# Hybrid decoder step on one core: gate tanh staged in three buffers, and the next weight block's low half made behind the first gate piece

## The reference, cut to what matters

```python
h = rmsnorm(x, norm_pre)
p = h @ w_in                               # 1088 tokens (1024 prompt, 64 sample), 3624 columns
y_conv = conv3(p.conv_c * p.conv_h)        # causal, depthwise, width 3, 256 channels
o_conv = p.conv_b * y_conv * silu(p.conv_z)
out = concat[nsa(p) * silu(z_nsa), gla(p) * silu(z_gla), o_conv] @ w_out
x = x + rmsnorm(out, norm_post)
```

## Time and profile before

| what | value |
|---|---|
| median of 3 runs | 958.06 us |
| lowest and highest | 951.75 and 960.32 us |
| span of the profiled execution, first to last instruction | 956.0 us |
| PE busy | 906.1 us (95% of the span) |
| DVE, ACT, POOL busy | 588.0, 421.0, 191.8 us |
| projection stage within the span | 0 to about 285 us |

### The profile page before, as it was taken

One profiled execution on the slowest core, in us unless ns is written; L12 is line 12 of the kernel. 1 busy time (PEld: TensorE's weight loads), 2 busy tenths in 40 slices (PEclk: granted clock), 3 DMA queues, 4 the chain that ended last, 5 costly groups with the idle time before them and its releaser, 6 DMA issues. The chain is left out here.

```text
span 956.0 us, 16677 instructions
## 1 busy us (share of the span) xinstructions
PE 906.1 (95%) x5935; PEld 796.0 (83%) x5935; DVE 588.0 (62%) x1396; ACT 421.0 (44%) x932; POOL 191.8 (20%) x179
## 2 busy tenths in 40 slices
PE   5999999997999999999999999997789999999997
PEld 4999999997989999988999998886355667777765
DVE  6432010058345567898866668897487788788663
ACT  6432221111113556777645657774373344434322
POOL 0029499999701000000000033000000000000000
PEclk9999999998998999999999999999698999999999
DMA  7227534543305211000011010431435365551411
GB/s 251 73 89 212 232 110 135 164 133 122 94 25 162 71 46 47 9 1 1 1 40 53 21 49 16 121 99 57 173 108 140 107 191 163 148 167 56 148 52 34
DMA packets 106820, 93.73 MB, mean 98 GB/s; under 512 B 21245, under 2 KB 99954, under 8 KB 104626
## 3 DMA queue, kind: packets, MB, share of 16 engines
q1 hardware_dynamic: 84946, 58.65, 20.5%
q10 hardware_dynamic: 19488, 17.25, 5.9%
q0 software_dynamic: 2304, 16.78, 5.1%
HBM read 78.16 MB, written 18.61 MB: 101 GB/s over the span
## 5 line engine op out<-in xcount | busy, mean ns | idle before, releaser
L660 PE MATMUL ps<-w_hi,h_hi 128*128 128x264 f32 (+5 forms) x432 | 124.1, 287 | 0.2 <-DVE h_lo L532 0.2
L660 PE MATMUL ps<-w_lo,h_hi 128*128 128x264 f32 (+5 forms) x432 | 123.1, 285 | 0.0
L660 PE MATMUL ps<-w_hi,h_lo 128*128 128x264 f32 (+5 forms) x432 | 123.0, 285 | 0.0
L540 DVE TENSOR_TENSOR w_lo<-w_raw,w_hi 128x1024 fp32r<-128x1024 f32 (+3 forms) x13 | 34.4, 2648 | 127.6 <-ACT w_hi L434 127.6
L1469 DVE TENSOR_REDUCE least<-ps 128x1 f32<-128x640 f32 (+7 forms) x128 | 89.8, 703 | 24.9 <-PE ps L1297 23.7
L1473 DVE TENSOR_TENSOR pt_lo<-ps,pt_hi 128x512 fp32r<-128x512 f32 x132 | 89.9, 686 | 17.2 <-ACT pt_hi L1405 15.6
L1405 ACT ACTIVATE pt_hi<-ps 128x512 fp32r<-128x512 f32 x132 | 78.2, 596 | 44.9 <-PE ps L1310 39.7
L381 POOL TENSOR_TENSOR chunk<-chunk 128x1024 f32<-128x1024 f32 (+2 forms) x46 | 82.4, 1792 | 3.6
L660 PEld LDWEIGHTS ps<-w_hi,h_hi 128*128 128x128 f32 (+1 forms) x432 | 79.7, 185 | 0.6 <-issue 0.4
L660 PEld LDWEIGHTS ps<-w_lo,h_hi 128*128 128x128 f32 (+1 forms) x432 | 79.8, 185 | 0.0
L660 PEld LDWEIGHTS ps<-w_hi,h_lo 128*128 128x128 f32 (+1 forms) x432 | 79.5, 184 | 0.0
(11 more groups left out here) (378 smaller groups left out, 2219.5 us busy)
## 6 DMA issues: line engine op xcount, KB each, us to landing
kv_pages<-in_cache_slc_kv SPq DMA_DIRECT2D x256, 64.0 KB, 1.9
shared<-in_x_prompt SPq DMA_DIRECT2D x8, 512.0 KB, 3.5
w_raw<-in_w_in SPq DMA_DIRECT2D x8, 512.0 KB, 3.9
wr_raw<-in_w_in SPq DMA_DIRECT2D x8, 512.0 KB, 4.3
kv_window<-in_cache_win_kv SPq DMA_DIRECT2D x4, 1024.0 KB, 5.8
wo_raw<-in_w_out SPq DMA_DIRECT2D x8, 512.0 KB, 8.4
out<-in_cache_win_kv SPq DMA_DIRECT2D x1, 4032.0 KB
x_row<-in_x_prompt ACTq DMA_DIRECT2D x7, 512.0 KB, 4.6
```

Of the source, the lines that this page charges most:

```text
L540: nc.vector.tensor_tensor(half(w_lo, b), raw(b), half(w_hi, b).bitcast(F32), ALU.subtract).then_inc(s_wlo, 1)
L660: mm = nc.tensor.matmul(out, lhs, rhs, start=(k == 0 and i == 0), stop=(k == KD - 1 and i == 2))
```

## The change

Three edits:

1. The tile `tanh` with its two buffers is gone. ACT writes tanh(z/2) into the three buffers of `stage`, by n % 3 of the gate piece n (0 to 5), and DVE works on it there.
2. ACT's wait: gate pieces 3 to 5 wait for the piece three before. Pieces 0 to 2 wait for all nine stores of block 5 out of that buffer (three each).
3. DVE's order in a block: for a z block only the first piece stands ahead of `split(b + 2)`, and the other two behind it. For h and b blocks the order stays. There are two z blocks, 8 and 12; a block 14 does not exist, so only block 8 has such a split, that of block 10.

```diff
--- before.py
+++ after.py
@@ -233,7 +233,6 @@
         w_lo = sb("w_lo", [P, 2, KD * WMAX], F32R)
         chunk = sb("chunk", [P, 2, CHT * 2 * ROW])
         stage = sb("stage", [P, 3, 364])
-        tanh = sb("tanh", [P, 2, 364])
         shared = sb("shared", [P, 3 * D])
         g_col = sb("g_col", [P, KD])
         stat = sb("stat", [P, 4])
@@ -458,9 +457,11 @@
                     elif what == "z":
                         t0, tn = CH3[t]
                         n = gate_no[x]
-                        if n >= 2:
-                            wait_taken(act, gates[n - 2])
-                        nc.scalar.activation(tanh[:, n % 2, 0:tn], ps[:, bank(x), 0:tn], ACT.Tanh, scale=0.5
+                        if n >= 3:
+                            wait_taken(act, gates[n - 3])
+                        else:
+                            act.wait_ge(s_st[n], 16 * ((len(staged) - n + 2) // 3))
+                        nc.scalar.activation(stage[:, n % 3, 0:tn], ps[:, bank(x), 0:tn], ACT.Tanh, scale=0.5
                                              ).then_inc(s_tanh, 1)
 
                 nc.scalar.preload_act_table_set("sqrt_and_others")
@@ -567,10 +568,10 @@
                     else:
                         n = gate_no[x]
                         dve.wait_ge(s_tanh, n + 1)
-                        did(nc.vector.scalar_tensor_tensor(tanh[:, n % 2, 0:tn], tanh[:, n % 2, 0:tn], 1.0, src,
+                        did(nc.vector.scalar_tensor_tensor(stage[:, n % 3, 0:tn], stage[:, n % 3, 0:tn], 1.0, src,
                                                            ALU.add, ALU.mult))
                         nc.vector.scalar_tensor_tensor(y_t[:, t0:t0 + tn], y_t[:, t0:t0 + tn], 0.5,
-                                                       tanh[:, n % 2, 0:tn], ALU.mult, ALU.mult
+                                                       stage[:, n % 3, 0:tn], ALU.mult, ALU.mult
                                                        ).then_inc(s_td, 1)
 
                 def conv(h):
@@ -617,12 +618,14 @@
                     if b == NB - 1:
                         dve.wait_ge(s_ct, 3)
                         nc.vector.tensor_copy(pq[HD:P, NT, 0:P], ps[HD:P, 7, 0:P]).then_inc(s_cn, 1)
-                    if b >= NTB:
-                        for x in prods:
-                            if x[0] == b and taken[x][0] == "dve":
-                                take(x)
+                    mine = [x for x in prods if x[0] == b and taken[x][0] == "dve"]
+                    first = 1 if kind(b) == "z" else len(mine)
+                    for x in mine[:first]:
+                        take(x)
                     if b + 2 < NB:
                         split(b + 2)
+                    for x in mine[first:]:
+                        take(x)
                     if kind(b) == "h":
                         conv(CHAN[b - NTB][1])
                     elif kind(b) == "b":
```

## The result

The changed kernel takes 948.67 us in the median of 9 runs (945.20 to 953.43), the kernel before 955.70 in 9 (951.21 to 960.32). The forecast's time was 950.2 us. The profiled execution has a span of 948.1 us, the number the sum gave, and a time of 949.82 us; so what lies around the span is 1.7 us.

The account below looks back on a forecast made before the run. TensorE, busy 95% of the span, was taken as the bound, so gains lay in its standstill and slow clock at block 10: −5.2 − 2.7 = −7.9 us, from 958.06 to 950.2 us; range 945.0 to 957.5.

Parts of the forecast that it names:

- the sum: Whole launch: span 956.0 − 7.9 = 948.1 us; from the median, 958.06 − 7.9 = 950.2 us, or −0.8%.
- The place and the size of the loss: TensorE at block 10, late in the projection: 5.2 us standstill plus 2.7 us slow clock, together 7.9 us, would go.
- the slow stretch: Behind the standstill, 232.6 to 238.8 us, TensorE's granted clock is 0.50, costing 2.7 us.
- Both parts are needed: Three tanh buffers ready block 10's high half by 217.3 us; the new order puts its split behind the first gate piece.
- The new wait for the stores of block 5: On ACT, the first gate pieces' tanh waits for stores issued before blocks 6 and 7; taken as 0 us.
- The split's end: VectorE's low half of block 10 ends at 225.2 us, at latest 226.8, ahead of TensorE's need at 227.5.
- What is late next: Block 11's split ends at 237.8 us, 1.7 to spare; the second convolution ends at 262 to 263.5, needed at 263.8.
- The wait that shrinks but stays: Rival, chance 0.14: block 10's split falls behind POOL's multiply, ends 1.8 us too late; 952.0 us, or 954.7 with slow clock.
- No loss in most launches: Rival, chance 0.15: engine order varies by launch, some have no gap at block 10; median 957 to 959 us.
- The convolution as the bound: Rival, chance 0.07: second convolution beside POOL takes 13.8 us, TensorE waits 6.4 before block 13, loses 2.7 to clock; 959.3 us.

Follow-up runs that it names:

- one copy more: Changed kernel with one PSUM copy of 364 elements between the first gate piece and block 10's split; no TensorE wait, stage ends at 277.29 us.
- the runs with a delayed split: Changed kernel with three or seven PSUM copies of 364 elements between the first gate piece and block 10's split; ratios to before 0.9939 and 0.9968.
- GpSimd late: Changed kernel with 13 memsets of 1024 elements on GpSimd ahead of its step 13; ratio to before 1.0055, stage ends at 286.54 us.

## Why the prediction was right

*The place and the size of the loss.* Right. 5.2 us of standstill and 2.7 of slow clock were foretold to go; the stage ended 8.2 us earlier. Of that, 0.15 us is a last block a little shorter (its last piece is taken 3.85 us behind the one before instead of 4.00); against the second profile of the kernel before it was 7.4 us, so how much of the slow stretch falls on matmuls is a thing of the single launch.

*Both parts are needed.* The text gave each its reason, and the two runs with one half each bore it out: a wait of 4.9 us with the buffers alone, 2.2 with the order alone, none with both. The new wait for the stores of block 5, taken at 0, cost nothing: the first tanh starts at 207.81, before at 207.80.

*The split's end.* Right by 0.3 us: 224.93 against 225.2. The reading behind it, that POOL's small add holds it and the gather issue then waits, is what the rows show (1.67 us for the issue). A smaller reading was wrong: the issue of 1.96 us at 211.81 was put down to the long convolution step, but that step starts at 213.15; the one beside it was the step before, from 211.63 to 212.91.

*What is late next.* I had 1.7 us to spare at block 11. There were 4.5: its split ended at 234.98, wanted at 239.5, since it came between two of POOL's adds and took 1.21 us, where I had taken 3.37. This time POOL was the one to wait: its three adds took 6.04 us there, 5.55 before. The second convolution ended at 261.4, where I had 262 to 263.5.

*The wait that shrinks but stays.* It did not happen in the two profiles of the changed kernel nor with one copy more. Its price was about right in the launch and a little low in its wait: the runs with a delayed split gave 2.2 and 2.4 us where I had 1.8, and ratios of 0.994 and 0.997, 952 to 955 us on the forecast's scale. The 1.8 came of counting the gather issue and the multiply from 223.4; by the earlier trace rows the multiply ends at 228.95, and a split behind it at 230.2, 2.7 us too late. The slow stretch, when it came, cost 1.7 us and not 2.7.

*No loss in most launches.* This rival falls. PE's wait was there in both profiles of the kernel before and in the buffers alone, at the same place and length. The spread of one kernel's times comes from elsewhere: the later stages took 670.9 and 666.5 us in two profiles of the changed kernel, with all of the projection alike.

*The convolution as the bound.* It was right that this decides the sign: with GpSimd late the launch took 1.0055 of the time before. The price I put on it was too low: 15.8 us of convolution where I had 13.8, and 7.4 us of wait where I had 6.4.

*The measured gain* of 7.0 us between medians is a little under the 7.9 of the profiles. The median of the kernel before fell from 958.06 in the 3 runs shown to 955.70 in 9 (954.57 and 954.80 in the 31 and 19 runs beside the experiments), which moved the base of the forecast and not its step. From the new base the sum would be 955.70 − 7.9 = 947.8 us, 0.9 below the measured 948.67; the recorded 950.2 is 1.5 above it.

## What to carry to other kernels

When a VectorE instruction takes several times its usual length (4.47 us for 0.54 here), look at GpSimd's timeline beside it. Where both engines read SBUF, their instructions take turns, and what matters is which gap between GpSimd's instructions an urgent one falls into. Put what TensorE waits for into the first gap, ahead of work that nobody waits for, and see to it that its input is there by then. Here the early input was worth nothing without the new place, and the new place without the early input missed the gap and left 2.2 us of the wait. A standstill of TensorE can cost more than its length: after 2.2 to 2.4 us a slow clock followed in two profiles of five, after 4.9 us and more in all four.

## What the runs showed of the hardware

The same standstill in the same kernel may or may not be followed by the slow clock. Two profiles of the changed kernel differ in the stretch behind the stage's end, though the wait at that end is 1.7 us in both (the next one, for a low half, is 0.7 and 0.4):

```profile
277.00:300.00 23.00, 22.17 (x142) 21.73 (x143) 13.57 (x34) 9.08 (x21) 5.64 (x21) 0.93 0.60 187
```

```profile
277.00:300.00 23.00, 22.41 (x153) 21.78 (x154) 13.79 (x35) 8.98 (x21) 5.72 (x21) 1.00 0.63 196
```

The granted clock there is 0.93 and 1.00. The times of one kernel spread with its mean granted clock. Of the 31 runs of the kernel before beside the first experiments, the four at 0.972 took 959.5 to 960.6 us and the two at 0.983 took 949.4 and 949.7. Which standstills of the later stages decide it was not tried.
